# Two-block kernel on one core: the first layer's products take x without its norm, the first weight unit comes in four pieces, and the decay table is computed in the first feed-forward layer

## What is computed

```python
def rmsnorm(x, w):
    xf = x.astype(jnp.float32)
    y = xf * lax.rsqrt(jnp.mean(xf * xf, axis=-1, keepdims=True) + NORM_EPS)
    return (y * w.astype(jnp.float32)).astype(x.dtype)
...
h = rmsnorm(x, norm_mix[i])
...
proj = h @ w_in                                   # q, k, v, g and the gate's low rank r
q, k, v, g, r = jnp.split(proj, [...], axis=-1)
logits = (r_dir @ w_up + b_up)
...
log_a = -LRU_C * r * jax.nn.softplus(-lam)        # recurrent mixer: depends on lam alone
```

## Time and profile before

| what | us |
|---|---|
| median of 3 runs | 863.88 (862.53 to 864.23) |
| the profiled execution, its own time | 861.99 |
| its span, first to last instruction | 860.2 |
| TensorE (PE) busy in it | 849.7 (99%) |
| VectorE (DVE) busy | 677.0 (79%) |
| ScalarE (ACT) busy | 542.6 (63%) |

### The profile page before, as it was taken

How to read it: one execution, slowest core, us unless ns; L and a number is a source line. 1 busy time by engine, 2 the same in 40 slices (tenths; PEclk the granted TensorE clock), 3 DMA queues, 4 the chain that set the end, 5 groups by cost and what they waited for, 6 DMA issues and landing times.

```text
span 860.2 us, 13361 instructions
## 1 busy us (share of the span) xinstructions
PE 849.7 (99%) x4881; PEld 746.8 (87%) x4881; DVE 677.0 (79%) x970; ACT 542.6 (63%) x746; POOL 38.8 (5%) x57
## 2 busy tenths in 40 slices
PE   8999999999999999999999999999999999999997
PEld 8988789888888888889888888989999898888886
DVE  6899668887877798868887886787977877776764
ACT  6855656757556566576666655578988775554533
POOL 1000100000000041000000000000010100000000
PEclk9999999999999999999999999999999999999999
DMA  7544534665554354224666655435363046655511
GB/s 276 203 170 178 198 140 151 236 234 207 212 211 163 144 178 165 99 99 149 242 216 246 224 199 207 154 127 216 135 250 155 1 154 239 234 182 193 219 50 50
DMA packets 22909, 152.82 MB, mean 178 GB/s; under 512 B 2608, under 2 KB 2736, under 8 KB 5712
## 3 DMA queue, kind: packets, MB, share of 16 engines
q1 hardware_dynamic: 22176, 149.45, 47.5%
q0 software_dynamic: 544, 2.49, 0.9%
q10 hardware_dynamic: 144, 0.26, 0.1%
HBM read 151.14 MB, written 1.05 MB: 177 GB/s over the span
## 4 chain that ended last, share of the span: by engine, by line
PE 87%; DVE 5%; ACT 1%; DMA 1%; issue 0%; POOL 0%; SPq 0%; ACTq 0%
PE acc L1863 26%; PE ring L1795 25%; PE ring L1799 13%; PE ring L1848 9%; PE ring L1810 4%; PE acc L2085 3%; PE ring L1829 2%; DVE w_lo L1005 2%; PE ring L2067 1%; PE ring L2243 1%; PE acc L1757 1%; PE ring L2125 1%; DMA raw<-in_stream_dram 1%; PE ring L2145 0%; PE acc L1883 0%; DVE la L1212 0%
## 5 line engine op out<-in xcount | busy, mean ns | idle before, releaser
L1005 DVE TENSOR_TENSOR w_lo<-raw,w_hi 128x2048 fp32r<-128x2048 f32 (+1 forms) x145 | 317.9, 2197 | 5.6 <-ACT w_hi L511 5.6
L511 ACT ACTIVATE w_hi<-raw 128x2048 fp32r<-128x2048 f32 (+1 forms) x146 | 267.0, 1840 | 51.6 <-DMA raw<-in_stream_dram 48.3
L1795 PE MATMUL ring<-hh,w_hi 128*128 128x512 f32 x944 | 235.7, 392 | 0.0
L1795 PEld LDWEIGHTS ring<-hh,w_hi 128*128 128x128 f32 x944 | 171.3, 189 | 31.7
L1799 PEld LDWEIGHTS ring<-hh,w_lo 128*128 128x128 f32 x944 | 128.8, 190 | 9.2
L1799 PE MATMUL ring<-hh,w_lo 128*128 128x256 f32 x944 | 131.6, 282 | 0.0
L1863 PE MATMUL acc<-w_hi,a_hi 128*128 128x512 f32 x264 | 103.8, 393 | 0.0
L1863 PE MATMUL acc<-w_lo,a_hi 128*128 128x512 f32 x264 | 103.1, 390 | 0.0
L1863 PE MATMUL acc<-w_hi,a_lo 128*128 128x512 f32 x264 | 102.8, 389 | 0.0
L1123 DVE TENSOR_TENSOR usum<-ring,usum 128x512 f32<-128x512 f32 x65 | 44.7, 688 | 58.9 <-ACT usum L516 58.6
L1848 PE MATMUL ring<-hh,w_hi 128*128 128x256 f32 x480 | 87.8, 285 | 0.0
(11 more groups left out here) (247 smaller groups left out, 961.9 us busy)
## 6 DMA issues: line engine op xcount, KB each, us to landing
raw<-in_stream_dram SPq DMA_DIRECT2D x134, 1024.0 KB, 4.8
raw<-in_stream_dram SPq DMA_DIRECT2D x12, 512.0 KB, 3.8
gatew<-in_gatew_dram POOLq DMA_DIRECT2D x4, 384.0 KB, 4.3
x<-in_x_dram SPq DMA_DIRECT2D x2, 512.0 KB, 3.8
out_dram<-xn SPq DMA_DIRECT2D x3, 256.0 KB, 2.6
row<-in_row_dram POOLq DMA_DIRECT2D x1, 640.0 KB, 4.1
gup_raw<-in_gup_dram SPq DMA_DIRECT2D x3, 128.0 KB, 11.2
par<-in_par_dram SPq DMA_DIRECT2D x1, 274.0 KB, 4.8
```

The costliest lines, as they stand in the source:

```text
L511: nc.scalar.activation(w_hi[:, u % RING, 0:n], raw[:, u % RAW, 0:n], ACT.Copy).then_inc(hi_split, 1)
L1005: nc.vector.tensor_tensor(w_lo[:, u % RING, 0:n], raw[:, u % RAW, 0:n], w_hi[:, u % RING, 0:n].bitcast(f32), ALU.subtract).then_inc(lo_spl ...
L1795: nc.tensor.matmul(ring[:, 2 * k + f, :], w_hi[:, u % RING, lo:lo + P], hh[:, kc, :, :], start=kc == 0, stop=False, skip_group_check=True)
```

## The change

The first layer's norm is taken out of the way of its products. TensorE transposes x itself; the products are scaled where they are copied out of PSUM: by `by_column` (the factor of each token along the free axis, the same in all partitions) for q, k and the rank product, by `first_rstd` (one factor per partition) for v and g. `by_column` is made by ScalarE spreading the factors (`by_token`), two TensorE transposes and a ScalarE copy. Unit 0 is loaded in four pieces of 512 columns and rounded piece by piece. The gamma columns of `par` come through ScalarE's own DMA queue, the rest of `par` later. TensorE spins 13, 3 and 7 transposes instead of 29, and the first products of q stand ahead of the rank products. The decay table becomes a function that VectorE calls in FFN 0, after the loop of steps 1 to 8 and before step 9; its instructions stay the same (cut here).

```diff
--- before.py
+++ after.py
@@ -141,8 +141,9 @@
 LO = KC + 1
-WARM = 29
-N_CONSTS = 2
+WARM = 13
+FILL = (3, 7)
+PIECES = 4
 COPIES = 3
...
@@ -375,10 +383,14 @@
                 sp.dma_start(x[:, t, :], x_in[0, t * P:(t + 1) * P, :]).then_inc(x_loaded[t], 16)
-            sp.dma_start(par[:, :], par_in).then_inc(consts_loaded, 16)
-            sp.dma_start(wr[:, :, :], wr_in.rearrange("p (c n) -> p c n", c=KC)).then_inc(consts_loaded, 16)
-            for u in range(RAW):
-                load(u)
+            for n in range(PIECES):
+                at = slice(n * UNIT // PIECES, (n + 1) * UNIT // PIECES)
+                signal = raw_loaded[0] if n == PIECES - 1 else piece_loaded[n]
+                sp.dma_start(raw[:, 0, at], stream[0:1, :, at].rearrange("o p n -> (o p) n")).then_inc(signal, 16)
+            sp.dma_start(wr[:, :, :], wr_in.rearrange("p (c n) -> p c n", c=KC)).then_inc(wr_loaded, 16)
+            load(1)
+            sp.dma_start(par[:, KC:N_PAR], par_in[:, KC:N_PAR]).then_inc(par_loaded, 16)
+            load(2)
             for c in range(COPIES):
...
@@ -583,16 +595,31 @@
 
-            for t in range(T):
-                act.wait_ge(x_loaded[t], 16)
-                sums(t, "mix0")
-            act.wait_ge(consts_loaded, 16 * N_CONSTS)
+            act.dma_start(par[:, 0:KC], par_in[:, 0:KC]).then_inc(gamma_loaded, 16)
+            act.wait_ge(x_loaded[0], 16)
+            sums(0, "mix0")
+            act.wait_ge(gamma_loaded, 16)
+            turned0("mix0")
+            for n in range(PIECES):
+                at = slice(n * UNIT // PIECES, (n + 1) * UNIT // PIECES)
+                last_piece = n == PIECES - 1
+                act.wait_ge(raw_loaded[0] if last_piece else piece_loaded[n], 16)
+                nc.scalar.activation(w_hi[:, 0, at], raw[:, 0, at], ACT.Copy).then_inc(hi_split if last_piece else piece_hi, 1)
+            act.wait_ge(wr_loaded, 16)
             nc.scalar.activation(copies(wr_hi), wr[:, :, :].unsqueeze(2).to_broadcast([P, KC, COPIES, 2 * GLA_RANK]),
                                  ACT.Copy).then_inc(wr_hi_ready, 1)
-            turned0("mix0")
-            split(0)
+            act.wait_ge(x_loaded[1], 16)
+            sums(1, "mix0")
             split(1)
-
+            act.wait_ge(made, 1)
+            for t in range(T):
+                act.wait_ge(rms_ready, RMS["mix0"] + t + 1)
+                nc.scalar.activation(by_token[:, t, :], ident[:, :], ACT.Identity, scale=0.0,
+                                     bias=first_rstd[:, t:t + 1]).then_inc(by_token_ready, 1)
+            act.wait_ge(column_turned, 1)
+            nc.scalar.activation(by_column[:, :], ring[:, 3, 0:S], ACT.Copy).then_inc(by_column_ready, 1)
+
+            act.wait_ge(par_loaded, 16)
             own.mark(nc.scalar.activation(lam_p[:, :], par[:, C_LAM:C_LAM + LRU_HEADS], ACT.Abs))
...
@@ -633,7 +660,7 @@
             for t in range(T):
-                nc.scalar.activation(v[:, t, :], acc[:, t, :], ACT.Copy).then_inc(v_ready, 1)
+                nc.scalar.activation(v[:, t, :], acc[:, t, :], ACT.Copy, scale=first_rstd[:, t:t + 1]).then_inc(v_ready, 1)
             for h in range(1, GLA_HEADS):
...
@@ -641,7 +668,7 @@
             for t in range(T):
-                nc.scalar.activation(sg[:, t, :], acc[:, t, :], ACT.Silu).then_inc(sg_ready, 1)
+                nc.scalar.activation(sg[:, t, :], acc[:, t, :], ACT.Silu, scale=first_rstd[:, t:t + 1]).then_inc(sg_ready, 1)
             for t in range(T):
...
@@ -1127,13 +1154,8 @@
 
-            for t in range(T):
-                dve.wait_ge(x_loaded[t], 16)
-                for half in range(2):
-                    normed("mix0", t, half)
-                if t == 0:
-                    dve.wait_ge(consts_loaded, 16 * N_CONSTS)
-                    front("mix0", 0)
+            dve.wait_ge(gamma_loaded, 16)
+            front("mix0", 0)
             for b in range(2):
...
@@ -1144,28 +1166,34 @@
             lower = slice(2 * GLA_RANK, 4 * GLA_RANK)
-            own.mark(nc.vector.tensor_copy(rt[:, :], ring[0:RANKS, GEN["rank"] % 4, 0:S]))
+            dve.wait_ge(by_column_ready, 1)
+            nc.vector.tensor_tensor(rank_scaled[:, :], ring[0:RANKS, GEN["rank"] % 4, 0:S], by_column[0:RANKS, :],
+                                    ALU.mult).then_inc(ring_free, 1)
+            dve.wait_ge(ring_free, 1)
+            own.mark(nc.vector.tensor_copy(rt[:, :], rank_scaled[:, :]))
             own.wait()
-            nc.vector.tensor_tensor(rt[lower, :], ring[lower, GEN["rank"] % 4, 0:S], rt[lower, :].bitcast(f32),
-                                    ALU.subtract).then_inc(ring_free, 1)
+            own.mark(nc.vector.tensor_tensor(rt[lower, :], rank_scaled[lower, :], rt[lower, :].bitcast(f32), ALU.subtract))
+            own.wait()
             dve.wait_ge(gup_hi_ready, 1)
 
+                both = by_column[:, :].unsqueeze(1).to_broadcast([P, 2, S])
                 if n < 2:
                     dve.wait_ge(used, U_Q + n + 1)
-                    nc.vector.tensor_scalar(qT[:, 2 * n:2 * n + 2, :], two(GEN["q"] + n), GLA_DK ** -0.5, None,
-                                            ALU.mult).then_inc(ring_free, 1)
+                    nc.vector.scalar_tensor_tensor(out=qT[:, 2 * n:2 * n + 2, :], in0=two(GEN["q"] + n), scalar=GLA_DK ** -0.5,
+                                                   in1=both, op0=ALU.mult, op1=ALU.mult).then_inc(ring_free, 1)
                 else:
                     dve.wait_ge(used, U_Q + n + 1)
-                    nc.vector.tensor_copy(kT[:, 2 * n - 4:2 * n - 2, :], two(GEN["q"] + n)).then_inc(ring_free, 1)
+                    nc.vector.tensor_tensor(kT[:, 2 * n - 4:2 * n - 2, :], two(GEN["q"] + n), both, ALU.mult).then_inc(ring_free, 1)
 
             evicted(1)
+            dve.wait_ge(par_loaded, 16)
             for d in range(2):
...
@@ -1176,31 +1204,6 @@
             split(4)
-            dve.wait_ge(lam_ready, 1)
-            own.mark(nc.vector.tensor_scalar(lam_q[:, :], lam_e[:, :], 2.0, None, ALU.add))
...
-            nc.vector.tensor_scalar(sp2[:, :], lam_p[:, :], LRU_C / 4, None, ALU.mult).then_inc(sp_ready, 1)
             split(5)
...
@@ -1256,6 +1259,34 @@
                 nc.vector.tensor_copy(far, ring[:, (g + 1) % 4, 0:T * P].rearrange("p (t c) -> p t c", t=T)).then_inc(ring_free, 1)
+
+            def lambda_table():
+
+                dve.wait_ge(lam_ready, 1)
+                own.mark(nc.vector.tensor_scalar(lam_q[:, :], lam_e[:, :], 2.0, None, ALU.add))
...
+                nc.vector.tensor_scalar(sp2[:, :], lam_p[:, :], LRU_C / 4, None, ALU.mult).then_inc(sp_ready, 1)
...
@@ -1371,6 +1402,8 @@
                 own.leave(FFN_ITERS // 2 - 1)
+                if n == 0:
+                    lambda_table()
                 step(FFN_ITERS - 2)
...
@@ -1909,17 +1942,21 @@
             pe.wait_ge(made, 1)
-            for _ in range(WARM):
-                nc.tensor.transpose(ring[:, 3, 0:P], ident[:, :], ident[:, :])
+            def spin(times):
+                for _ in range(times):
+                    nc.tensor.transpose(ring[:, 3, 0:P], ident[:, :], ident[:, :])
+
+            spin(WARM)
             for t in range(T):
-                turn("mix0", t)
-            pe.wait_ge(wr_hi_ready, 1)
+                pe.wait_ge(x_loaded[t], 16)
+                for kc in range(KC):
+                    last = nc.tensor.transpose(turned_at("mix0", t, kc), x[:, t, kc * P:(kc + 1) * P], ident[:, :])
+                    if kc % 4 == 3:
+                        last.then_inc(x_turned, 1)
+                spin(FILL[t])
             def rank(a, c):
                 for kc in range(KC):
-                    if (a, c) == (0, 0):
-                        for t in range(T):
-                            has_high("mix0", t, kc)
                     last = nc.tensor.matmul(ring[0:RANKS, GEN["rank"] % 4, 0:S], (wr_hi, wr_lo)[a][:, kc, :], h_parts[c][:, kc, :],
...
@@ -1927,6 +1964,13 @@
                 for kc in range(KC):
+                    if (u, a, c) == (U_Q, 0, 0):
+                        for t in range(T):
+                            has_high("mix0", t, kc)
+                        if kc == KC - 2:
+                            pe.wait_ge(hi_split, U_Q + 1)
+                        elif kc % 2 == 0:
+                            pe.wait_ge(piece_hi, kc // 2 + 1)
                     if (u, c) == (U_Q, 1):
...
@@ -1935,15 +1979,19 @@
 
-            rank(0, 0)
-            pe.wait_ge(hi_split, U_Q + 1)
             product(U_Q, GEN["q"] % 4, 0, 0)
             product(U_Q, GEN["q"] % 4, 0, 1)
+            pe.wait_ge(wr_hi_ready, 1)
+            rank(0, 0)
             rank(0, 1)
+            ready(U_Q)
+            product(U_Q, GEN["q"] % 4, 1, 0).then_inc(used, 1)
             pe.wait_ge(wr_lo_ready, 1)
             rank(1, 0).then_inc(filled, 1)
-            ready(U_Q)
-            product(U_Q, GEN["q"] % 4, 1, 0).then_inc(used, 1)
+            pe.wait_ge(by_token_ready, T)
+            for t in range(T):
```

(16 more changed lines are left out.)

44 lines of the change are left out of this document (22 added, 22 removed).

## The result

The changed kernel takes 865.27 us (median of 22 runs, 864.16 to 869.07) beside 862.97 (22 runs, 861.81 to 864.66): ratio 1.0029, 95% interval 1.0022 to 1.0035. That is 2.3 us slower by the medians and 2.5 by the ratio. The profiled execution has a span of 862.5 and 864.59 us as its own time.

A forecast was written before the change was run, and what follows sets the result against it. TensorE, busy for 99% of the span, was taken as the bound, so only its waits and non-product work pay. Front -1.3 and table +1.9 give 0.6 us more: 863.88 + 0.6 = 864.5, range 861.9 to 866.3.

The forecast's parts named there:

- within 0.2%: Whole kernel: a time that measurement can't tell from no change, 0.2% being 1.73 us; chance 0.64.
- the first rival: Opening: the clock rises at about 5 instead of 7.06, front gains 2.4 to 2.7 us, total 863.1; chance 0.15.
- The pieces: Opening, ScalarE's queue: four roundings of unit 0 end near 9.5, before the last product pair needs them at 9.9.
- the wait of 0.7 for w_lo near 14.4: Opening: TensorE wants unit 0's low part at 14.4, VectorE has it at 15.07, so TensorE waits 0.7 us.
- ScalarE behind TensorE: Opening: by_column's copy waits for transposes until 18.55; unit 2 starts at 25.75 instead of 26.31, leaving 0.55 of 2.3 us.
- Copies out with a scale: Copies of q, k, v and g: zero cost, at most 0.1 us each, beside TensorE's work.
- Later in GLA: Waits at 67.88 and the third head's scores go; load of unit 15 and GLA's last transposes come 1.3 us early.
- The table: FFN 0: the table's 5.08 us on VectorE delays step 9; TensorE stands 1.9 us ahead of down(10).
- cover found: FFN 0: down(10) doesn't stall because TensorE's earlier work is longer, so -1.3 us (862.6); chance 0.12.
- The sum: Whole kernel: 861.99 - 1.3 + 1.9 = 862.6, 0.6 us more; from the median 863.88, forecast 864.5.
- the front: Opening to the end of GLA, with the later waits removed: gains 1.3 us.
- slower: Opening: by_column's copy, transposes and wake-ups take 0.6 us more and cost the head start; 865.2 to 865.6; chance 0.18.

The follow-up runs named there:

- after_again: The changed kernel measured once more with no edit; ratio 1.0023 to the kernel before.
- front_only: The changed kernel with the decay table back at its old place between the splits of units 4 and 5; ratio 1.0015 to the kernel before.
- table_chunks: The changed kernel with the decay table cut into five pieces called in attention, none in FFN 0; ratio 1.0013 to the kernel before.
- gup_early: The changed kernel with ScalarE's rounding of gup moved ahead of its copy of by_column; ratio 1.0025 to the kernel before.
- gup_load: The changed kernel with gup rounded ahead of by_column and its three loads issued ahead of par's rest and unit 2; ratio 1.0012 to the kernel before.
- table_only: The kernel before with only the decay table moved to FFN 0, between the loop and step 9; ratio 1.0012 to the kernel before.
- whole_unit: The changed kernel with unit 0 loaded whole instead of in four pieces, still rounded in four parts; ratio 1.0022 to the kernel before.
- all_four: The changed kernel with unit 0 whole, gamma behind x on SyncE, gup loaded and rounded earlier, table in pieces in attention; ratio 1.0000 to the kernel before.
- best_pieces: The changed kernel with gup loaded ahead of unit 2, rounded ahead of by_column, and the table in pieces in attention; median 861.91 beside 862.27, ratio 0.9998.

## Why the prediction was right or wrong

The time of 865.27 lies in the range (861.9 to 866.3) and the sign of the forecast is right. Its size is not: 2.3 us more than before, where I had 0.6, so that "within 0.2%" had most of the chance (0.64) and a slowdown of 0.29% came, which had 0.19. That the time itself was forecast to 0.8 us (864.5) is in part luck: I started from 863.88, the median of three runs, and 22 runs of the same kernel gave 862.97. The base was 0.9 too high and the change 1.7 too small.

- **The clock.** It rose at 4.91 in the profile after, at 7.55 in after_again, and between 4.27 and 7.38 in eleven other kernels' profiles: the condition of the first rival. Its gain did not come. VectorE's `low` started 0.9 us earlier than forecast (7.89 against 8.78), although x landed at 4.43 and not at 4.20, but TensorE then waited for rounded pieces. A later fall of the clock, which the forecast doesn't have, may stand behind the longest executions: in 4 of the 22 (866.45, 867.86, 868.16 and 869.07 us) the mean granted clock is 0.996 or 0.997, in the others 0.998 to 1.000. Without them the median is 865.1, so it isn't the 2.3 us.
- **The pieces: the step that failed.** "The pieces ... end near 9.5": they ended at 10.61, and at 11.36 in the same program. I priced their rounding and took their loads as free. In the profile after this ate the gain of the early clock and no more: the low products start at 15.06, where I had 15.15, and the wait of 0.7 for w_lo near 14.4 didn't come, because TensorE had lost that time already. In front_only and table_chunks the pieces came 0.6 and 0.75 later still, and unit 2 with them.
- **ScalarE behind TensorE.** Forecast: transposes done at 18.55, unit 2 at 25.75; measured 18.34 (when ScalarE starts the copy behind them) and 25.61. gup_early and gup_load show the mechanism. The chain was right, and lacked a link: 1/rms of the second tile, on GpSimd, behind VectorE's w_lo. It costs 0.38 of the 0.99 us that after_again is behind at unit 2.
- **Copies out with a scale.** Put at zero and beside TensorE's work; each of the four ScalarE instructions takes 0.09 longer. At v that is 0.18 on TensorE, at `sg` 0.17 in the chain of waits.
- **Later in GLA.** The load of unit 15 was 1.28 early, as forecast (1.3), but the end of GLA 0.98, and 0.24 in after_again, and 0.18 late in table_chunks. A mean near 0.35 is my estimate from these three. Of the 0.95 that it lacks against 1.3, 0.43 are lost up to unit 2 (0.70 early, 0.29 and 0.05 late: a mean of 0.12 instead of 0.55), 0.17 between there and the load of unit 15, which the longer copy of v explains, and 0.35 behind that load, half from `sg` and half from how long it took (4.95, 4.70 and 5.37 us). The part that the table's move gives, 0.45 + 0.3, measured 0.74 in table_only, where no copy is scaled.
- **The table.** 1.9 forecast, 1.87 measured, and 1.84 to 1.87 in the six other profiles that have it there. Rival "cover found" falls.
- **The losses behind FFN 0.** Not in the sum. FFN 1's first down product and the short-convolution mixer have no margin for a unit that lands late (in the second place 6.7 us from issue to landing in the changed kernel, 5.1 in the kernel before): 0.2 and 0.9 us in the changed kernel, 0 and 0 in after_again, -0.1 and 0.6 in front_only. The kernel before has the same places. Whether the new front makes late units more frequent, or these profiles caught them, isn't settled.
- **The sum.** With the front at 0.35, the table at 1.87 and 0 to 1.1 later, it is 1.5 to 2.6 us, around the measured 2.3. Which of the later losses belong to the change stays open. The rival "slower" had the right time (865.2 to 865.6), but only with the base that was 0.9 too high, and by another mechanism than the one that I named: `by_column`'s own copy was priced right.

## What to carry to other kernels

Work on the start of a kernel is paid only down to the slowest supplier: read the loads' rate and the queues behind each new wait (here ScalarE's rounding of gup behind the copy of `by_column`, and GpSimd's small sums behind VectorE's large ones) before counting a head start. Price a scale that is added to a copy, too. A chain of small instructions belongs where its engine waits anyway, in pieces, not ahead of work with a margin of zero. Where one profile shows a gain and the runs don't, compare the spread of the runs: 11 cheap spins came with 1.5 us less of median there, for a reason that no profile shows. And take the base of a forecast from more than three runs where they differ by more than the change is worth.

## What the runs showed of the hardware

- Four loads of 2 KB rows at the stream's start moved 161 to 226 GB/s between 5.5 and 7.5 us, in eight profiles, and later pieces of them 380; a load of whole 8 KB rows moved 413 in the same stretch (whole_unit).
- A GpSimd addition of one column (128x1) took 0.19 us alone, and 1.87, 4.86 or 5.08 beside VectorE's two-input w_lo.
- A ScalarE copy or activation of 128x1024 elements took 1.02 us, and 1.11 with one factor per partition as its scale.
- TensorE's clock can fall back while it is busy, after a wait of 3.3 us: 3.4 us at 1.2 GHz in all_four.
- The same 1 MB load at the same place took between 4.7 (best_pieces) and 6.6 us (gup_load) to land.
